# A block's gate-weight sums on VectorE, moved in front of the recurrence's second step

## The reference

```
mod = silu(c) @ w_ada + b_ada;  shift, scale, gate = split(mod, 3)
h = rms_norm(x) * (1 + scale) + shift
xr, gr, qc, kvc, kr, ga = split(h @ w_in)
xc = causal depthwise conv of width 4 over xr
r, i = sigmoid(blockwise xc @ w_rg_a + b), sigmoid(blockwise xc @ w_rg_x + b)
a = exp(-8 * r * softplus(-lambda));  b = sqrt(1 - a*a) * (i * xc)
y_rnn = scan(h_t = a_t * h_(t-1) + b_t) * silu(gr)
y_att = latent attention(qc, kvc, kr), 8 heads, * silu(ga)
x = x + gate * (concat(y_rnn, y_att) @ w_out)
```

## Time and profile before

| | |
|---|---|
| median of 3 runs | 2464.42 us (2463.91 to 2464.75) |
| the profiled execution | 2466.64 us, its span 2464.9 us |
| mean granted clock of TensorE | 0.989 |
| busy, share of the span | TensorE 98%, GpSimd 40%, VectorE 38%, ScalarE 34% |
| the chain that ended last | TensorE 89%, VectorE 5% |

### The profile page before, as it was taken

The page is one execution under the profiler, slowest core; times in us unless marked ns, Lnnn a source line. Parts: engine busy times, 40 slices in busy tenths (PEclk is TensorE's granted clock), DMA queues, the critical chain, the costliest instruction groups (busy, mean ns, idle before and its releaser), DMA issues.

```text
span 2464.9 us, 28185 instructions
## 1 busy us (share of the span) xinstructions
PE 2404.6 (98%) x11092; PEld 1902.9 (77%) x11092; DVE 927.3 (38%) x1485; ACT 834.5 (34%) x1283; POOL 984.2 (40%) x426
## 2 busy tenths in 40 slices
PE   7899998999999999999999999999999999999996
PEld 4567676777888888887787778787878888888885
DVE  4764466466500520210555534343421412202113
ACT  5245344452322432222434333333322312213321
POOL 1344333234455534443332324242434444444553
PEclk9899999999999999999999999999999999999998
DMA  8962233235444343333222323232333444454332
GB/s 297 402 243 80 61 119 114 91 105 188 156 152 141 126 161 96 88 101 90 66 85 60 94 82 107 86 109 84 107 96 101 154 147 129 131 166 122 93 103 85
DMA packets 98435, 309.03 MB, mean 125 GB/s; under 512 B 10624, under 2 KB 12032, under 8 KB 98176
## 3 DMA queue, kind: packets, MB, share of 16 engines
q1 hardware_dynamic: 98304, 307.23, 38.9%
HBM read 285.17 MB, written 20.97 MB: 124 GB/s over the span
## 4 chain that ended last, share of the span: by engine, by line
PE 89%; DVE 5%; ACT 2%; DMA 2%; issue 2%; SPq 1%; POOL 0%; DVEq 0%; ACTq 0%; POOLq 0%
PE bank L535 24%; PE bank L538 24%; PE bank L536 24%; PE bank L531 2%; PE bank L534 2%; PE bank L532 2%; PE bank L1044 2%; PE bank L1068 1%; PE bank L1056 1%; DVE hlo L1729 1%; DMA raw<-in_wst 1%; PE bank L829 1%; PE bank L840 1%; DVE hlo L2449 1%; DMA rawx<-in_wst 1%
## 5 line engine op out<-in xcount | busy, mean ns | idle before, releaser
L2517 POOL TENSOR_TENSOR wlo<-raw,whi 128x1024 fp32r<-128x1024 f32 x365 | 894.0, 2455 | 1248.0 <-ACT whi L1161 1215.0
L535 PE MATMUL bank<-hhi,whi 128*128 128x512 f32 x2752 | 1088.1, 395 | 19.2 <-ACT whi L1161 16.5
L538 PE MATMUL bank<-hhi,wlo 128*128 128x512 f32 x2752 | 1078.5, 392 | 7.3 <-POOL wlo L2517 7.3
L536 PE MATMUL bank<-hlo,whi 128*128 128x512 f32 x2752 | 1075.9, 391 | 0.0
L535 PEld LDWEIGHTS bank<-hhi,whi 128*128 128x128 f32 x2752 | 518.9, 189 | 144.5 <-ACT whi L1161 18.2
L538 PEld LDWEIGHTS bank<-hhi,wlo 128*128 128x128 f32 x2752 | 518.2, 188 | 123.2 <-POOL wlo L2517 13.1
L536 PEld LDWEIGHTS bank<-hlo,whi 128*128 128x128 f32 x2752 | 518.9, 189 | 107.1 <-issue 0.7
L1161 ACT ACTIVATE whi<-raw 128x1024 fp32r<-128x1024 f32 x365 | 384.5, 1055 | 587.9 <-PE bank L538 481.9
L2325 DVE TENSOR_SCALAR S<-S,sm 128x512 f32<-128x512 f32 (+1 forms) x64 | 78.0, 1219 | 0.6
L1594 ACT ACTIVATE S<-S,sm 128x512 f32<-128x512 f32 (+1 forms) x64 | 35.3, 551 | 119.0 <-DVE sm L2315 119.0
L534 PE MATMUL bank<-wlo,hhi 128*128 128x512 f32 x192 | 74.8, 390 | 0.7 <-POOL wlo L2517 0.7
(11 more groups left out here) (308 smaller groups left out, 2098.4 us busy)
## 6 DMA issues: line engine op xcount, KB each, us to landing
raw<-in_wst SPq DMA_DIRECT2D x397, 512.0 KB, 3.6
rawx<-in_wst SPq DMA_DIRECT2D x54, 512.0 KB, 6.7
rawy<-in_wst SPq DMA_DIRECT2D x26, 512.0 KB, 3.7
tgs<-TS SPq DMA_DIRECT2D x32, 256.0 KB, 3.8
axr<-tgs SPq DMA_DIRECT2D x32, 256.0 KB, 4.0
X<-in_xt SPq DMA_DIRECT2D x4, 1024.0 KB, 14.8
pls<-stg SPq DMA_DIRECT2D x16, 256.0 KB, 9.4
axr<-in_xt SPq DMA_DIRECT2D x16, 256.0 KB, 2.8
```

The source lines that it names most:

```text
L535: e.matmul(o, hi, xh, start=first, stop=False)
L536: e.matmul(o, hi, xl, start=False, stop=False)
L538: return e.matmul(o, lo, xh, start=False, stop=last)
L2517: e.tensor_tensor(sub(wlo, PAIR[c], CH), slots[slot(c)], sub(whi, PAIR[c], CH).bitcast(F), ALU.subtract).then_inc(*up("wlo_pool", "wlo", c))
```

## The change

In the block loop of VectorE's program the third tick and the block's gate sums change places. Before, VectorE does: convolution (tick 2), second step of the recurrence and score copies (tick 3), sums of the block's two gate chunks, product of the gate `gr` (L2135), scan (tick 4). After, the sums stand between convolution and second step. No other engine's program changes.

```diff
@@ vector(e), for c in range(8) @@
                 gate_columns()
                 jobs.insert(0, recurrence(c))
                 tick()
-                tick()
                 for _ in range(GATED[2 * c] + GATED[2 * c + 1]):
                     next(gate_it)
+                tick()
                 w.wait_ge(*done("gr", c))
```

## The result

The changed kernel takes 2449.07 us (median of 4 runs, 2446.20 to 2450.78) against 2464.59 us before (4 runs, 2463.91 to 2467.27), a ratio of 0.9934 with a 95% interval of 0.9917 to 0.9951. Run again on another occasion it took 2448.08 against 2465.33 us, ratio 0.9925 (0.9912 to 0.9937). The forecast was 2446.5 us, inside a range of 2444.7 to 2453.8.

What follows compares the result with a forecast made beforehand. TensorE, busy 98% of the span, was taken as the bound. Gains of 10.30 us (block 3) and 7.63 (block 7), together 17.93, brought the profiled 2466.64 to 2448.7; less 2.2 gave 2446.5 us, range 2444.7 to 2453.8.

Steps and rivals of the forecast that it cites:

- The bound: Whole kernel: TensorE, busy 98% of the span, bounds it; its waits at `L880` for `gac` total 11.4 us in two.
- The cost of a stall: Blocks 3 and 7: stretches lose 11.20 and 8.53 us, through waits of 6.7 and 4.7 us plus slow clock.
- the terms of the sum: Losses less 0.90 us per visit (eight `L880` products): block 3 gains 10.30, block 7 gains 7.63, together 17.93 us.
- The new place: VectorE, between convolution and second step: four sums take about 3.5 us, hidden in 5.99 us of idle time.
- The room of 2.4 + 5.2 us: Block 3: sums end 2.4 us before the second step can start; score copies have another 5.2 us before value products.
- The queues: SyncE: `rawy` slots free earlier, next loads go out from about 413.8; loads needing split-freed slots move little; worth nothing.
- Clock falling at the visit itself: TensorE's eight `L880` products lower the clock anyway, each visit costing 4.54 us, not 0.90: 2453.8 us; chance 6%.
- Long sums: VectorE's four sums take up to 2.93 us each in the new place, delaying the copies: 2451.3 us; chance 5%.
- One wait left: Only one `L880` wait goes; block 7 keeps its own because something else is late: 2454.1 us; chance 4%.
- no effect: What TensorE needs next in place of `gac` is as late in both blocks: 2464.4 us; chance 5%.
- slower by late chunks: VectorE held at the sums by chunks not landed, delaying value products; 2470.5 us at 3 us beyond; chance 4%.
- taken off that, 2446.5 us: Last step: profiled 2466.64 us becomes 2448.7; the profiled execution's 2.2 us above the median is taken off.

Runs made afterwards that it cites:

- only3: Kernel before with the gate sums moved ahead of the second step in block 3 alone: 2455.99 us against 2465.33, ratio 0.9954.
- only37: Kernel before with the gate sums moved in blocks 3 and 7 alone: 2447.90 us against 2465.33, ratio 0.9929.
- others: Kernel before with the gate sums moved in the six blocks other than 3 and 7: 2467.79 us against 2465.33, ratio 1.0002.
- one_chunk: Kernel before with only one of each block's two gate chunks summed ahead of the second step: 2460.49 us against 2465.67, ratio 0.9976.
- visit_late: Kernel before, VectorE unchanged, TensorE's eight `L880` products put into the middle of the next projection: 2450.21 us against 2465.67, ratio 0.9938.
- pad4: Changed kernel plus eight value-preserving VectorE passes over `gac` in each of eight blocks: 2448.23 us; kernel before 2465.67, ratio 0.9930.
- pad6: Changed kernel plus twelve value-preserving VectorE passes over `gac` in each of eight blocks: 2474.95 us; kernel before 2465.67, ratio 1.0036.

## Why the prediction was right

**The bound.** The share of TensorE and its two waits at `L880` were the right thing to read. only3, only37 and others show that the gain lies in the two blocks that have these waits; one_chunk and visit_late tie it to the waits themselves.

**The cost of a stall.** A waiting time of 11.4 us was priced at 17.9 us because of the clock. The stretches of the changed kernel show 10.3 and 7.6 us, the terms of the sum to the tenth. one_chunk shows from the other side that a wait costs more than its length: 6.1 us of waiting cost 11.4.

**The new place.** Forecast: sums some 3.5 us long, 2.4 us before the second step. Measured: 3.55 and 2.53. The room of 2.4 + 5.2 us is bracketed by pad4, which fits with 0.5 us to spare, and pad6, which doesn't.

**The queues.** Each of the next `rawy` loads goes out as soon as its slot's sums are done, as forecast. That the weight loads behind them "move little" was wrong: in block 3 they went out at 428.72 and 429.20 before and go out at 417.25 and 424.96 now, 13.0 and 5.8 us earlier relative to TensorE. Only the second was bound to a GpSimd split; the first had been held by nothing but the late `rawy` loads ahead of it in SyncE's order. It made no difference to the time, since TensorE waited for none of these weights. ScalarE's split that had waited 7.2 us for a load starts at 548.72 without such a wait, and relative to the end of TensorE's last `win1` projection of block 7 it is 7.3 us earlier (2.5 us behind ScalarE's `L1451` of block 7, before 9.8). A wait of 2.3 us for a load is left at ScalarE's next `rawy` split, and TensorE does not wait for it.

**The rivals.** Clock falling at the visit itself: it did not, in four visits of the changed kernel. Long sums: block 3's first one, begun inside a split, took 1.12 us, the other three 0.75 each, 3.55 in all. One wait left, no effect, or slower by late chunks: none occurred; VectorE has no idle time in front of `gac`.

**What was mis-sized** is the last step, "taken off that, 2446.5 us", with its own range of 2445 to 2448 "since the runs shown lie within 0.8 us of each other". The measured time lies outside that range and inside the wide one. Three runs of before were too few to show what an execution's opening does, and the profiled execution, at 2466.64, already lay 1.9 us above the highest of them: the 15 runs of before that stand beside the run again go from 2464.70 to 2469.79, and the traces' first `L829` from 303.7 to 308.6 us, with identical instructions ahead of it. The measured 2449.07 us is 2.6 above the forecast: two of its four runs are at 2450.78, one of them the profiled one with its late opening, and the others at 2446.20 and 2447.35. That the openings account for the spread of the runs without a trace is likely and not shown. The mechanism's size, 17.9 us, was right; as a difference of medians it came out as 15.5 in these runs and 17.3 in the next.

## What to carry to other kernels

When the bounding engine waits for a helper's result, look at where the result stands in the helper's queue before making it faster: here four instructions moved into an idle time in front of another wait took away 11.4 us of waiting. Price a TensorE stall by the stretch, not by the wait: the slow clock behind it added more than half again, and with the waits cut in half, 5.3 of its 6.5 us stayed. And only the places where something is waited for count; moving the same work in the six other blocks gave nothing.

## What the runs showed of the hardware

**The clock after short waits.** In one_chunk TensorE waited 3.1 us at each of the two visits, and the granted clock fell behind both (0.95 and 0.91 in the stretches). In visit_late a wait of 1.3 us and eight small products were followed by slow value products (4.10 us against 2.32). Eight small products with no wait ahead of them had this effect in none of the visits of the changed kernel, of only37 or of pad4: their stretches are at 1.00.

**The opening.** The same instructions reach the first `L829` between 303.7 and 308.6 us. The granted clock from 60 to 110 us goes with it: it was 0.83 and 0.86 in the traces with 306.9 us or more, 0.90 in the one with 306.2, and 0.93 in those with 303.7 to 304.8. In only37, one of these:

```profile
60.00:110.00 50.00, 42.61 (x243) 28.18 (x246) 38.52 (x57) 15.38 (x23) 15.30 (x6) 0.93 1.02 392
```

**VectorE and GpSimd hold each other.** A sum begun inside a split was known to be held until the split's end. The changed kernel shows the other direction too. GpSimd's timeline in block 3:

```profile
422.50 2.39 POOL L2517 TENSOR_TENSOR wlo<-raw,whi 128x1024 fp32r<-128x1024 f32 x1 [8.68 <-ACT whi L1161]
426.88 3.14 POOL L2517 TENSOR_TENSOR wlo<-raw,whi 128x1024 fp32r<-128x1024 f32 x1 [1.99 <-ACT whi L1161]
```

The second split begins at 426.88, inside the scan that VectorE started at 426.61 and that takes 1.22 us, and lasts 3.14 us; before, the one that began at 425.36, only 0.2 us before a sum's end, took 2.37. VectorE's next product, begun at 427.94 inside that split, takes 2.62 us in place of 0.69. It looks as if whichever engine comes second waits for the other's instruction; this was read off the traces and not isolated. It is in line with the contention of which the Trainium skill speaks in "GPSIMD Engine Reference", Key points: the scan and the product both read two tensors from SBUF. VectorE's `L2135` at 423.85, which reads one of its two tensors from a PSUM bank, took 0.69 us inside the split begun at 422.50; before, outside any split, it took 0.67. Here both delays are hidden.
